# Projection pieces set between the small products of three steps of a chunked recurrence

## The reference

```python
h = x * (1 + sc1) + sh1
p = h @ w_in[l]                      # 1024 -> 512 + 3*1024 + 288 + 2*1024 columns
...
xs = ps + (token_shift(ps) - ps) * mu
r, k, v, xw, xa, xg = jnp.split(xs, SHIFT_SPLITS, axis=-1)
...
def step(state, inp):                # one token; 16 heads of 64
    r_t, w_t, k_t, v_t, a_t, b_t = inp
    sa = jnp.einsum('bhvk,bhk->bhv', state, a_t)
    state = (state * w_t[:, :, None, :] + sa[..., None] * b_t[:, :, None, :]
             + v_t[..., None] * k_t[:, :, None, :])
    return state, jnp.einsum('bhvk,bhk->bhv', state, r_t)
```

## Time and profile before

| | |
|---|---|
| three runs | 1053.32, 1057.69, 1067.57 us; median 1057.69 |
| profiled execution | 1054.66 us, its span on the core 1053.0 us |
| busy in the span: PE, DVE, ACT, POOL | 968.5, 665.7, 474.3, 380.9 us |
| mean granted clock of TensorE | 0.980 |

### The profile page before, as it was taken

One profiled execution on the slowest core, in us unless ns is written; L12 is line 12 of the kernel. 1 busy time (PEld: TensorE's weight loads), 2 busy tenths in 40 slices (PEclk: granted clock), 3 DMA queues, 4 the chain that ended last, 5 costly groups with the idle time before them and its releaser, 6 DMA issues.

```text
span 1053.0 us, 27456 instructions
## 1 busy us (share of the span) xinstructions
PE 968.5 (92%) x11539; PEld 805.0 (76%) x11539; DVE 665.7 (63%) x925; ACT 474.3 (45%) x579; POOL 380.9 (36%) x222
## 2 busy tenths in 40 slices
PE   1898899999999999899999999798999999999993
PEld 1676677786778678677688888688899898898993
DVE  7326478577847857754232255567778787777877
ACT  0545345346435632435423242374545546345451
POOL 8333411411331132124453454245154252361542
PEclk9999999999999999999999999898999999999997
DMA  9332334224232423432453418213241341423201
GB/s 363 123 94 65 93 94 125 64 82 127 89 89 82 143 63 90 115 89 61 127 136 108 145 59 256 58 43 102 79 139 57 102 134 46 139 82 95 63 1 80
DMA packets 122918, 108.03 MB, mean 103 GB/s; under 512 B 5395, under 2 KB 104641, under 8 KB 122817
## 3 DMA queue, kind: packets, MB, share of 16 engines
q1 hardware_dynamic: 112720, 83.37, 26.5%
q10 hardware_dynamic: 10097, 23.16, 7.3%
HBM read 100.23 MB, written 2.10 MB: 97 GB/s over the span
## 4 chain that ended last, share of the span: by engine, by line
PE 72%; DVE 15%; ACT 5%; issue 3%; POOL 2%; DMA 1%; SPq 1%; ACTq 0%; DVEq 0%; POOLq 0%
PE bank L1873 13%; PE set L2235 11%; PE bank L2321 7%; PE set L2174 6%; PE bank L2174 5%; PE set L1927 4%; PE set L2321 4%; PE set L2273 3%; PE set L1915 3%; PE set L1939 3%; PE bank L2235 2%; PE bank L1854 2%; PE set L1951 1%; DVE a_sum L1518 1%; DVE w_lo L1559 1%
## 5 line engine op out<-in xcount | busy, mean ns | idle before, releaser
L660 POOL TENSOR_TENSOR w_lo<-w_raw,w_hi 128x1024 fp32r<-128x1024 f32 (+2 forms) x75 | 171.1, 2281 | 381.8 <-ACT w_hi L770 373.3
L770 ACT ACTIVATE w_hi<-w_raw 128x1024 fp32r<-128x1024 f32 (+2 forms) x81 | 81.8, 1010 | 103.8 <-PE set L2174 35.2
L819 ACT ACTIVATE Q<-set 128x1024 f32<-128x1024 f32 x56 | 57.5, 1027 | 133.5 <-PE set L1927 70.3
L1873 PE MATMUL bank<-h_hi,w_hi 128*128 128x512 f32 x256 | 106.8, 417 | 5.0 <-POOL w_lo L660 3.3
L1605 DVE SCALAR_TENSOR_TENSOR res<-set,mod,res 128x256 f32<-128x256 f32 x192 | 92.9, 484 | 25.8 <-PE set L2235 17.1
L2235 PE MATMUL set<-a_hi,w_hi 128*128 128x256 f32 x384 | 109.2, 284 | 0.0
L2235 PE MATMUL set<-a_lo,w_hi 128*128 128x256 f32 x384 | 108.9, 283 | 0.0
L2235 PE MATMUL set<-a_hi,w_lo 128*128 128x256 f32 x384 | 108.8, 283 | 0.0
L1146 ACT ACTIVATE w_hi<-w_raw 128x1024 fp32r<-128x1024 f32 x70 | 74.3, 1062 | 69.8 <-PE set L2235 64.3
L1873 PE MATMUL bank<-h_lo,w_hi 128*128 128x512 f32 x256 | 102.4, 400 | 1.5 <-issue 1.5
L1873 PE MATMUL bank<-h_hi,w_lo 128*128 128x512 f32 x256 | 102.0, 398 | 0.0
(11 more groups left out here) (361 smaller groups left out, 2285.1 us busy)
## 6 DMA issues: line engine op xcount, KB each, us to landing
w_raw<-in_w_ff_dram SPq DMA_DIRECT2D x64, 512.0 KB, 4.0
w_raw<-in_w_in_dram SPq DMA_DIRECT2D x46, 512.0 KB, 3.7
y<-in_w_ada_dram ACTq DMA_DIRECT2D x20, 512.0 KB, 3.7
ada<-in_w_ada_dram SPq DMA_DIRECT2D x16, 512.0 KB, 10.1
Q<-in_w_ada_dram ACTq DMA_DIRECT2D x12, 512.0 KB, 4.1
w_raw<-in_w_rwkv_up_dram SPq DMA_DIRECT2D x8, 512.0 KB, 3.7
w_raw<-in_w_out_dram SPq DMA_DIRECT2D x8, 512.0 KB, 4.5
xtok<-in_x_dram SPq DMA_DIRECT2D x4, 512.0 KB, 6.7
```

Of the source, the lines that this page charges most:

```text
L660: link(pool.tensor_tensor(part_of(k, w_lo), raw_part(k), part_of(k, w_hi).bitcast(F32), ALU.subtract), "lo_ready")
L770: link(act.activation(part_of(k, w_hi), raw_part(k), ACT.Copy), "hi_ready")
L819: link(act.activation(by_half(tile), psum_flat(set_of(name)), ACT.Copy), "act_kept")
L1873: mm = pe.matmul(o, w, hx, start=(m == 0), stop=(m == 3 * KT - 1))
```

## The change

In steps 0, 8 and 19 of the four full iterations some of the step's pieces are issued between its small products. As many are taken from those behind it, so that every step has as many pieces as before, and their sequence (chunk and part) is the same.

```diff
+            BETWEEN = {0: 2, 8: 2, 19: 1}
...
                         to_pairs("TB", it, [(c7, IB)])
+                        gemm_piece()
                         pe.wait_ge(sem("bk_made"), 2 * it + 2)
                         to_pairs("TK", it, [(c8, IB)])
+                        gemm_piece()
...
                         to_heads("A8T", it, [(b1, b2)])
+                        gemm_piece()
                         wait_kept(pe, "D1", it)
                         wait_kept(pe, "A4I", it)
                         to_heads("D2", it, [(std(b4), b7)])
+                        gemm_piece()
...
                     both_to_heads("MR1", it, b1, c3, c7)
+                    gemm_piece()
                     to_heads("N", it, [(c3, b2), (c4, c5)])
...
-                for _ in range(pieces_in(it, s)):
+                for _ in range(pieces_in(it, s) - (BETWEEN.get(s, 0) if work else 0)):
                     gemm_piece()
```

## The result

| | before | after |
|---|---|---|
| executions | 1050.98, 1053.32, 1057.69, 1067.57 us | 1064.97, 1068.71, 1078.47, 1080.74 us |
| median | 1055.51 us | 1073.59 us |
| profiled execution, its span | 1054.66 us, 1053.0 us | 1078.47 us, 1076.8 us |
| mean granted clock in it | 0.980 | 0.964 |

The changed kernel takes 1.0149 times as long, 95% interval 1.0106 to 1.0192: slower by 11 to 20 us. The forecast was 1061 us and its range ended at 1069. The sign was right and the size was not.

The account below looks back on a forecast made before the run. TensorE, busy 968.5 of 1053.0 us, was taken as the bound. Borders +5.1, shift wait +6.8, POOL wait +1.0 and closed gaps -6.9 gave +6.0 on 1054.66: forecast 1061 us, range 1053 to 1069.

Parts of the forecast that it names:

- Part 1: Steps 0, 8 and 19: 16 more borders between small and large matmuls, +5.1 us.
- Part 2: Step 8, iterations 0 to 2: the first piece waits for VectorE's shift, 2.27 us each, +6.8 us.
- Part 3: Step 0 of iteration 0: TensorE idles for POOL with TK still to do, +1.0 us.
- Part 4: Instruction-supply gaps close in steps 0, 8 and N while OI's grow: -6.9 us.
- rival D: The idle at step 8's shift wait also costs clock, two or three falls, +3 to +5: 1064 to 1066 us; chance 0.12.
- B: Faster than before: more gaps close and half-clock stretches return to full clock, 1052 us; chance 0.15.
- E: VectorE's shift in step 8 comes early enough, so its wait vanishes: 1054 us; chance 0.05.
- C: The instruction gaps stay or only move to the next border: +12.9, 1067.6 us; chance 0.12.

Follow-up runs that it names:

- 4: The whole change, with VectorE issuing the shift of step 7 ahead of its copy of A8T: 1061.75 us, 1.0046 times the kernel before.
- 7: The kernel before, no piece moved, with TensorE made to wait behind A8T for VectorE's shift in iterations 0 to 2: 1073.98 us, ratio 1.0138.
- 1: The kernel before with only step 8's pieces moved: 1068.3 us, ratio 1.0140.
- 11: The whole change, but step 8 of iteration 3 left as in the kernel before: 1068.42 us, ratio 1.0109.
- 9: The kernel before plus the wait on the shift, filled with ten unused large matmuls: 1065.36 us, ratio 1.0067.
- 10: The whole change with ten unused large matmuls between A8T and step 8's first piece, iterations 0 to 2: 1073.17 us, ratio 1.0127.
- 12: The whole change with ten unused large matmuls filling each shift wait, and step 8 of iteration 3 as before: 1070.65 us, ratio 1.0107.
- 8: The kernel before with only step 8's pieces moved, one product later, behind D2 and W0: 1068.04 us, ratio 1.0094.
- 2: The kernel before with only step 0's pieces moved: 1058.96 us, ratio 1.0017.
- 6: VectorE's shift issued first, step 8's pieces moved, step 0's from iteration 1 on, step 19's left: 1056.53 us, ratio 0.9989.

## Why the prediction missed

**The sum was right, for what it summed.** It said +6.0 us; the full part measured +6.9. Step by step:

- Part 1 (borders, +5.1): the product between two pieces takes 1.10 us as forecast. With step 8's wait out of the way (4) the full part is +1.5, where 5.1 + 1.0 - 6.9 = -0.8 was to be left; the wait on line 1306, 5.1 us in place of 2, accounts for about the difference.
- Part 2 (the shift, +6.8): 6.9 us in three waits of 2.29. The rows of VectorE before were enough to place it to a tenth.
- Part 3 (POOL, +1.0): the wait is 2.49 us, from 1.27.
- Part 4 (gaps, -6.9): "issue" fell from 12.0 to 5.6 us, none is left in step 8 or in N, and those in OI grew by 2.1 us (0.85 to 1.45 in iteration 3), where +2.0 was forecast from a supply of 128 matmuls a block. What I missed is that closing the gap of 1.9 us in step 8 of iteration 3 gives next to nothing: `yT`, five steps on, waits for VectorE's line 1267, and that wait grew by 1.3 us, from 2.2 to 3.5; the two borders there take the rest. The prediction called TensorE "the engine that never has any" idle time to catch up in, and at `yT` it was VectorE that set the pace. The prediction also counts five gaps within a product; by its rows and line 1927's six gaps in the earlier trace rows there are seven.

**What failed is the price of rival D.** Of the 12.6 us between the forecast and the median, 0.9 are the sum's. The clock is the largest term, some 7.9 us, and the forecast put it at nothing. Under "the idle of part 2 costs clock as well" stood "a fall costs some 1.6 us: two or three give +3 to +5", a chance of 0.12, and nothing of it in the forecast. Measured, the withheld clock rises by some 8 us (32.5 against 24.6) with the change and by 9.4 ± 2.8 with the wait alone. There were two errors in it. I priced a fall by the three stretches of the trace before, 3.4 us each; there are stretches of 13.6 and 17 us too, at the waits of `yT` of 3.3 to 4.2 us, and once behind a wait of 0.83. And I took the one gap of 2.17 us without a fall behind it as a reason against, where in 7 three waits of 2.2 us do it. The Trainium skill, page "TensorE: Matmul & The Clock Gate", section A second HAM failure mode: psum-queue depth-cycling, tells of another kernel, in bf16, whose TensorE idles briefly between groups of matmuls, so often that its clock goes up and down. I had not weighed that. The result of 7 points the same way, 34.0 us withheld beside 24.6, though it adds three waits and not frequent ones.

**The base was low.** The rest, 3.9 us between means, is the base: the sum was added to the profiled execution, 1054.66 us, where the 73 executions of the kernel before have a mean of 1058.6. From that mean the same sum gives 1064.6, still 9 us short, so it isn't the base that failed.

**Against the rivals.** B (faster) and E (the shift early) fall with part 2. C (1067.6 us) has the nearest number, but for a reason that the trace refutes, since the gaps did go. D has the mechanism, at about half its size.

**What stays open.** That holding TensorE up in step 8 costs clock, over the time of the wait, is shown: 7 does it with no piece moved, and steps 0 and 19 alone don't. How much of it is the standing itself is not settled. Taking the kernels with the standing wait together (the change, 1, 7, 11: 18 executions), 31.5 ± 1.5 us are withheld; with the wait filled or removed (4, 9, 10, 12: 32 executions) 28.2 ± 0.8; before, 24.6 ± 0.5. The difference of 3.3 ± 1.7 us would be about half of the loss, but it is under two standard errors, and the grouping was made after the results.

Two other waits account for part of the rest. TensorE's wait on line 1306 in iteration 0 is 1.9 to 2.0 us in nine traces, and the half-clock stretch at it is 3.4 us long in each; it is 4.3 to 5.2 us in the other five (4, 8, 10, 11, 12), and the stretch is 6.8 us in each. And all six traces with the wait of 2.5 us on GpSimd in step 0 (the change, 2, 4, 10, 11, 12) have a half-clock stretch of 3.4 us at it, while none of the eight with 1.3 us or less has one. By half a stretch of 3.4 us each, my estimate is 1.7 us of clock for either, 3.4 together, where 4, 10 and 12 have 2 to 6 us over the kernel before. The longer waits at `yT` in iteration 3 are a third candidate. No kernel removed all three and kept the pieces of step 8 and the wait on the shift.

## What to carry to other kernels

When an edit makes the bound engine wait in the middle of small products, count the wait itself and expect a loss of clock on top (here 6.6 to 6.9 us of waits came with 6.9 ± 1.6 us of clock, over the 18 executions with it; no other kernel was measured), and prefer to take the wait away by issuing its producer earlier on the other engine, or not to move the work at all. To judge such a change, split each execution's span into span times granted clock and the rest: the first part told the sum of this change within 1 us from four executions, where the times themselves differed by 16; the second part needs many executions, since four gave it only to 4 us. A gap that closes is a gain only if no other engine's result is waited for a little further on.

## What the hardware showed that I had not expected

- Three waits of 2.2 us, 6.6 us in 1066, lengthened the kernel by 1.38% (0.91 to 1.86), some 15 us.
- Half-clock stretches come in a few lengths: 3.4 us mostly, also 6.8 and 10.2, and 13.6 or 17.1 us at waits of 3.3, 3.5 and 4.2 us of the same product, `yT` (1, the change, 10). But behind a wait of 2.2 us there 11 has 3.4 us and 12 has 10.2, and at ones of 3.2 and 3.3 us kernels 4 and 6 have 3.4: the length of the wait alone doesn't decide.
- The same wait can have a stretch behind it or not: all six of 2.5 us on GpSimd have one, three of the twelve of 2.2 to 2.3 us on the shift.
- The supply of TensorE's own instructions seems to limit a run of small products: where two "issue" gaps follow each other closely, in N and OI of iterations 1 and 3, there are 128 matmuls from one to the next, and the gaps are 12.0 us in all before and 5.6 with large matmuls in between.
- VectorE took 2.20 us for 128x8 elements while a GpSimd operation of 3.16 us ran, and 0.17 us where that operation began 0.15 us later than it.
